# Gate matmuls placed between wide matmuls, and value-tile splits on VectorE alone, in a hybrid PEER decoder block

## The reference, cut to what matters

```python
def chunk(xc):                                     # xc: 128 tokens
    q = (xc @ w_q).reshape(TOKEN_CHUNK, PEER_HEADS, 2, half)
    s = jnp.einsum('thpd,hpnd->thpn', q, sub_keys)
    top_s, top_i = lax.top_k(s, PEER_TOPK)         # 16 best of 128 keys, twice
    cand = top_s[:, :, 0, :, None] + top_s[:, :, 1, None, :]
    best_s, best_c = lax.top_k(cand.reshape(...), PEER_TOPK)
    ...
    e = i1 * PEER_N_KEYS + i2                      # expert of 128 x 128
    gate = jax.nn.softmax(best_s, axis=-1)
    h = jnp.einsum('thkd,td->thk', u_tab[e], xc)
    act = jax.nn.gelu(h, approximate=False) * gate
    return jnp.einsum('thk,thkd->td', act, v_tab[e])
```

## Time and profile before

| | before |
|---|---|
| median of 3 executions | 1195.76 us (1192.87 to 1197.58) |
| profiled execution, span | 1195.7 us |
| TensorE busy | 1175.6 us, 98% |
| VectorE busy | 752.9 us, 63% |
| ScalarE busy | 510.1 us, 43% |
| GpSimd busy | 507.7 us, 42% |
| DMA | 181.91 MB, mean 152 GB/s |

### The profile page before, as it was taken

How to read it: one execution, slowest core, us unless ns; L and a number is a source line. 1 busy time by engine, 2 the same in 40 slices (tenths; PEclk the granted TensorE clock), 3 DMA queues, 4 the chain that set the end, 5 groups by cost and what they waited for, 6 DMA issues and landing times.

```text
span 1195.7 us, 21882 instructions
## 1 busy us (share of the span) xinstructions
PE 1175.6 (98%) x7850; PEld 1087.5 (91%) x7850; DVE 752.9 (63%) x1232; ACT 510.1 (43%) x798; POOL 507.7 (42%) x216
## 2 busy tenths in 40 slices
PE   8999999999999899999999999999999999999998
PEld 6998989999999899999999999988888888888887
DVE  5467776530898994544343433677787776767675
ACT  6444666454544445333333233333333333444443
POOL 3644444655567766522322233232233332444442
PEclk8999999999999999998988899898999989999999
DMA  5753344444455354444333433333433333555552
GB/s 200 268 183 124 126 141 159 159 146 173 159 175 174 129 189 176 142 141 140 118 118 115 140 123 123 124 128 135 140 137 126 139 123 126 191 193 193 193 193 106
DMA packets 52258, 181.91 MB, mean 152 GB/s; under 512 B 5851, under 2 KB 9051, under 8 KB 52092
## 3 DMA queue, kind: packets, MB, share of 16 engines
q1 hardware_dynamic: 52220, 181.41, 44.3%
HBM read 177.97 MB, written 3.41 MB: 152 GB/s over the span
## 4 chain that ended last, share of the span: by engine, by line
PE 88%; DVE 10%; issue 1%; ACT 1%; DMA 0%; SPq 0%; ACTq 0%; DVEq 0%
PE bank L1047 41%; PE bank L1319 30%; PE bank L1277 10%; PE bank L1128 2%; DVE lo L322 2%; DVE act L885 1%; PE bank L1057 1%; DVE act L880 1%; PE bank L1141 1%; PE bank L1255 1%; DVE act L887 1%; DVE ohA L962 1%; DVE prob L747 0%; DVE act L861 0%; DVE act L856 0%
## 5 line engine op out<-in xcount | busy, mean ns | idle before, releaser
L322 POOL TENSOR_TENSOR lo<-raw,hi 128x1024 fp32r<-128x1024 f32 x202 | 504.7, 2503 | 673.1 <-ACT hi L309 672.7
L309 ACT CAST hi<-raw 128x1024 fp32r<-128x1024 f32 x332 | 348.1, 1049 | 260.6 <-PE bank L1319 249.5
L1047 PE MATMUL bank<-nrm_hi,hi 128*128 128x256 f32 x1504 | 441.2, 293 | 9.9 <-DVE lo L322 7.7
L1047 PE MATMUL bank<-nrm_lo,hi 128*128 128x256 f32 x1504 | 436.6, 290 | 0.0
L1047 PE MATMUL bank<-nrm_hi,lo 128*128 128x256 f32 x1504 | 436.1, 290 | 0.0
L1047 PEld LDWEIGHTS bank<-nrm_hi,hi 128*128 128x128 f32 x1504 | 300.5, 200 | 15.4 <-issue 10.5
L322 DVE TENSOR_TENSOR lo<-raw,hi 128x1024 fp32r<-128x1024 f32 x130 | 171.4, 1318 | 206.5 <-ACT hi L309 206.1
L1047 PEld LDWEIGHTS bank<-nrm_lo,hi 128*128 128x128 f32 x1504 | 300.5, 200 | 0.1
L1047 PEld LDWEIGHTS bank<-nrm_hi,lo 128*128 128x128 f32 x1504 | 299.9, 199 | 0.0
L982 DVE TENSOR_TENSOR nrm_lo<-act,nrm_hi 128x256 fp32r<-128x256 f32 x128 | 142.2, 1113 | 105.1 <-ACT nrm_hi L597 105.1
L572 ACT ACTIVATE act<-bank 128x256 f32 x128 | 49.2, 384 | 284.8 <-PE bank L1047 284.6
(11 more groups left out here) (172 smaller groups left out, 784.2 us busy)
## 6 DMA issues: line engine op xcount, KB each, us to landing
raw<-u_tiles SPq DMA_DIRECT2D x128, 512.0 KB, 3.3
raw<-v_tiles SPq DMA_DIRECT2D x128, 512.0 KB, 3.2
raw<-front SPq DMA_DIRECT2D x76, 512.0 KB, 3.3
toeplitz<-prob SPq DMA_DIRECT2D x12, 192.0 KB, 4.3
bias<-toeplitz SPq DMA_DIRECT2D x12, 128.0 KB, 4.3
resid<-x_t SPq DMA_DIRECT2D x2, 512.0 KB, 4.7
qk<-sub_keys SPq DMA_DIRECT2D x1, 1024.0 KB, 6.6
y<-act SPq DMA_DIRECT2D x2, 512.0 KB, 2.6
```

The costliest lines, as they stand in the source:

```text
L309: act_e.copy(hi[:, s, :], raw[:, s, :]).then_inc(hi_ready, 1)
L322: eng.tensor_tensor(lo[:, s, :], raw[:, s, :], hi[:, s, :].bitcast(F32), ALU.subtract)\
L1047: ins = pe.matmul(dst, w_[:, s, u * P:(u + 1) * P], x_[:, k, :], start=first and i == 0 and p_ == 0, stop=last and i == n - 1 and p_ == 2)
```

## The change

Three edits. The 16 matmuls of a gate group are issued one by one between the wide matmuls of one tile: group 0 in the iteration's first tile, group 1 in its third. In a u tile a gate follows the first and the second of every three wide matmuls. In a v tile one gate precedes each wide matmul, and two precede each of the first four. VectorE's `multiply` moves from places 0 and 2 to places 1 and 3, ahead of the `one_hots` there. And `by_dve` gives VectorE the low part of every v tile from the fourth on; GpSimd's last loop ends with the third v tile.

```diff
+G_VALUES = N_FRONT + N_U + LEAD
...
-            return slot_of(base, j) == 3 or (base + j >= G_SHARED and slot_of(base, j) == 1)
+            return (slot_of(base, j) == 3 or (base + j >= G_SHARED and slot_of(base, j) == 1)
+                    or base + j >= G_VALUES)
...
-            for base, tiles in ((U0 + LEAD, HALF), (G_SHARED, N_U + N_V - RING - HALF)):
+            for base, tiles in ((U0 + LEAD, HALF), (G_SHARED, HALF)):
...
-                    if j % 2 == 0:
+                    if j % 2 == 1:
                         multiply(half, it, j // 2)
-                    elif not last:
-                        one_hots(half, it, 2 + j // 2)
+                        if not last:
+                            one_hots(half, it, 2 + j // 2)
...
+            def gate_part(half, it, g, r):
+                if r == 0:
+                    pe.wait_ge(spread, it * 4 + (half * GROUPS_N + g) * 2 + 2)
+                q, i = divmod(r, 2)
+                ins = pe.matmul(bank[6 + g][:, q * HALF:(q + 1) * HALF], ohA[:, g, :, q], ohB[:, g, i, :, q],
+                                start=i == 0, stop=i == 1, skip_group_check=True)
+                if r == 2 * TOK - 1:
+                    ins.then_inc(gate_mm, 1)
...
+                for k in range(KB):
+                    for p_, (w_, x_) in enumerate(((hi, nrm_hi), (hi, nrm_lo), (lo, nrm_hi))):
+                        ins = pe.matmul(dst, w_[:, j, k * P:(k + 1) * P], x_[:, k, :], start=k == 0 and p_ == 0,
+                                        stop=k == KB - 1 and p_ == 2, skip_group_check=True)
+                        if k == KB - 1 and p_ == 2:
+                            ins.then_inc(pe_step, 1)
+                        elif gates and p_ < 2:
+                            gate_part(0, it, j // 2, 2 * k + p_)
...
             def u_and_gates(it):
-                gates(0, it)
                 for j in range(RING):
-                    u_tile(HALF, it, j)
+                    u_tile(HALF, it, j, gates=j % 2 == 0)
...
                         for half in range(2):
+                            for _ in range((2 if c == 0 and a_ is nrm_hi else 1) if gates else 0):
+                                gate_part(1, it, j // 2, done_gates)
+                                done_gates += 1
                             ins = pe.matmul(bank[2 * c + half][:, :], a_[:, j, c * P:(c + 1) * P],
...
             def v_and_gates(it):
-                gates(1, it)
                 for j in range(RING):
-                    v_tile(0, it, j)
+                    v_tile(0, it, j, gates=j % 2 == 0)
```

More of the change, by code:

```diff
@@ L1261, in _, with u_tile @@
                     freed(pe, job)
-            def u_tile(base_i, it, j):
-                wait(pe, gelu_done, it * 4 + (base_i + j - 1))
[L1266 to L1279, removed]
+            def gate_part(half, it, g, r):
[6 more added lines that the diff above has]
+                    ins.then_inc(gate_mm, 1)
+            def u_tile(base_i, it, j, gates=False):
+                wait(pe, gelu_done, it * 4 + (base_i + j - 1))
+                wait_lo(pe, U0 + base_i, it, j)
+                dst = bank[4 + j % 2][:, 0:T]
+                for k in range(KB):
[6 more added lines that the diff above has]
+                            gate_part(0, it, j // 2, 2 * k + p_)
             for j in range(RING):
@@ L1308, in _, with v_tile @@
                 u_and_gates(it)
-            def v_tile(base_i, it, j, stop=False):
+            def v_tile(base_i, it, j, stop=False, gates=False):
                 wait_lo(pe, V0 + base_i, it, j)
                 pe.wait_ge(a_hi, it * 4 + (base_i + j + 1))
+                done_gates = 0
                 for c in range(TC):
```

## The result

The changed kernel takes 1203.66 us (median of 6, 1201.15 to 1208.75), the kernel before, in the same comparison, 1195.67 (1192.52 to 1197.87): ratio 1.0081, 95% interval [1.0058, 1.0103]. It is 0.8% slower. The forecast was 1159 us, range 1140 to 1183; both missed. The time is that of the fourth rival, 1204, which had a chance of 0.07.

The account below looks back on a forecast made before the run. The prediction took TensorE, busy 98% of the span, as the bound, its clock lowered by gate bursts. Terms: 1195.7 - 20.1 - 17.0 + 1.2 - 0.5 = 1159.3 us, forecast 1159, range 1140 to 1183.

Parts of the forecast that it names:

- the fourth rival: Gate tiles: each change of matmul kind stalls 0.025 us, 45 us in all, 1204 us; chance 0.07 together with late VectorE.
- The prey: Both gate stretches: after bursts TensorE's clock falls and wide matmuls pay about 1.5 us; excess 20.1 us in u, 17.0 in v.
- The rule of the Trainium skill: Gate stretches: idle gaps, not bursts, lower the clock, so spreading gates brings nothing; 1196 us, chance 0.04.
- What a gate costs in its new place: Gates between wide matmuls: a pair costs the wide's time and 0.12 to 0.13 us, as now; net 0.
- The first rival: V tiles with gates: gates nearly free between wide matmuls, 0.05 us instead of 0.123, 37 us more gained, 1122; chance 0.10.
- The signs: Profile with gates: clock 1.00, iterations about 15.5 us (u) and 14.9 (v), GpSimd silent after three v tiles, 1.2 us gap.
- Where the stages meet: Stage borders: 1.2 us of idle added before the first v tile; a wait of about 0.5 us at 1018.40 goes.
- VectorE alone: V tiles: VectorE takes over GpSimd's splits, hidden by TensorE, cost 0; uncovered it would be 3.7 us per gate tile.
- The moved `multiply`: VectorE's queue: `multiply` in place 1 waits for a group ending with tile 0; the work behind isn't due yet, cost 0.

Follow-up runs that it names:

- both groupings: The changed kernel with each tile's 16 gates in four blocks of four (1167.47 us), or each group of 16 whole ahead of its tile (1161.7 us).
- the grouped kernel: The changed kernel with each group of 16 gates standing whole ahead of its tile: 1161.7 us, ratio 0.9718 to the kernel before.
- the packed columns: The changed kernel with each gate's 128 float16 weight columns read side by side instead of 16 bytes apart: 1163.23 us, ratio 0.9725.

## Why the prediction was wrong

*The prey was read rightly.* The bursts cost the clock, and without bursts of 32 it stays at 1.00, or at 0.99 in the v half: the changed kernel and both groupings show it. 37 us of excess were read from the earlier trace rows; the grouped kernel gave back 267.5 - 247.6 = 19.9 us in u (20.1 foretold) and 255.1 - 241.1 = 14.0 in v (17.0 less 1.2 foretold; 1.6 of the difference is the slow first tile). The rule of the Trainium skill that stood against it, page "TensorE: Matmul & The Clock Gate", section "HAM oscillation — how this bites in real kernels", does not describe the falls of the kernel before: the clock fell with TensorE never idle, and stayed up when only the order of its work was changed (the runs with one burst and with groups of 16). The one fall that is left in the groups of 16 does stand behind a gap.

*The step that failed* is "What a gate costs in its new place": "a gate after a wide is covered", pair = wide plus 0.12 to 0.13, net 0. Measured: (273.1 - 247.4)/512 = 0.050 us more a gate in u, and (259.9 - 238.1 - 1.2)/512 = 0.040 in v, where a quarter of the gates stand behind another gate. In all 25.7 + 20.6 = 46 us, against 37 regained. I had bounded the extra at 9 us, from the gate-to-wide edge alone (0.13 for 0.12). The other edge stood in the same rows, the late first load with its 0.26 us idle, and I put it down to the semaphore wait. The gates inside a tile, which have no wait, behave the same. That the late load is paid in full, the packed columns show: a load shorter by 0.050 us made the gate cheaper by 0.050.

*The fourth rival had the mechanism and, in part by luck, the size.* It foresaw that loads of one kind aren't put behind matmuls of the other, at 0.025 a change of kind, 45 us; the runs give 46. That the rate came from two waits at the ends of a burst and fits so closely is luck: at the ends of blocks of four it is about half. The rival was too vague in what "kind" is: float16 by itself goes ahead (the run with 96 columns); the fast load does not. The Trainium skill, page "TensorE: Matmul & The Clock Gate", section "What happens when you issue a matmul", says that a weight load is pulled ahead of matmuls in flight if the row groups don't conflict or if it goes to the background buffer. The trace agrees for the wide loads and the plain float16 load, and shows no pull ahead for the fast one (645.16, not 645.04). Which buffer a load goes to no trace here tells.

*The first rival* fell too: the cheapest gate of any run took 0.107 us, not 0.05.

*The signs.* The clock, the silent GpSimd, the one-hots and the gap before the first v tile came as foretold. The iterations did not: 273.1/16 = 17.1 us in u for 15.5, 259.9/16 = 16.2 in v for 14.9. The sign for the fourth rival, above 17 us at full clock, showed in u alone.

*Where the stages meet* was right in place: TensorE is idle 1.16 us before the first v tile (1.2 foretold), and the wait of 0.5 us at the middle of the v tiles is gone (174.9 to 174.1; 174.7 where GpSimd keeps its splits).

```profile
763.95 1.16 issue
765.11 0.41 PE bank L1270 x2
```

*VectorE alone* was right at cost 0: two pairs of runs with and without it agree (1203.66 and 1204.27, 1161.7 and 1160.93). VectorE's busy time even fell, 168.49 us for 192.87 in the v stretch, since its one-hots no longer run beside GpSimd's splits: the instruction that took 1.79 us on average takes 0.68. In the run that differs only in GpSimd keeping its splits it takes 2.90, and VectorE is busy 198.66 us (first the changed kernel, then that run).

```profile
L967 DVE TENSOR_TENSOR ohB<-eqB,parts 128x1024 f16<-128x1024 f16 x30 | 20.5, 683 | 0.0
...
L966 DVE TENSOR_TENSOR ohB<-eqB,parts 128x1024 f16<-128x1024 f16 x30 | 86.9, 2896 | 0.0
```

*The moved `multiply`* at cost 0 was right too: no wait for a one-hot shows in the changed kernel, and the run with one burst, which keeps the move, is equal to before.

## What to carry to other kernels

Where a stretch of small matmuls costs TensorE's clock, try shorter stretches before single instructions. Here two bursts of 16 gave back 34 of the 37 us that 32 interleaved gates promised, with one edge each. Before interleaving two sorts of matmul, look at the load side of both edges: if the load of one sort starts only when the other's columns are through, each alternation pays that load in full, as here, and a wait that happens to stand there must be told apart from it by an instruction without one. And where such a load is exposed, its length matters, so look at how its columns lie.

## What the runs showed that was not expected

- A float16 load of 128 columns (the fast mode) starts 0.12 us after a 256-column matmul starts, one of 96 columns (plain) with it. Why the fast one isn't put ahead is not settled; four chunks and a full 128 columns were not told apart.
- The fast load takes 0.14 us with columns 16 bytes apart, 0.10 side by side; the plain one of 96 spread columns sets a gate at 0.176 us, longer than a gate with 128 columns (0.123). Why the spacing changes the length was not tried.
- Between wide u matmuls, gates with plain float32 loads cost 0.107 us each, less than in any burst of float16 gates (0.116 and 0.123).
- A burst of 16 left the clock up, except where 1.16 us of idle stood before it. How much each of the two adds was not tried.
- A VectorE write of 1024 float16 elements spread 256 bytes apart takes 4.8 us, 6.7 times the dense one.
